# When the three expert loads into freed buffers are issued at the turn from mixer to experts

## The reference, cut to what matters

```python
for l in range(DEPTH):                      # DEPTH = 2
    ...
    x = x + merged @ w_out[l]
    x = x + hier_moe(rmsnorm(x, norm_ffn[l]), ...)

# hier_moe: 32 experts, top-1 group of 8, then the top 2 experts in it, per token
def expert_block(args):
    xb, e = args
    return (jax.nn.silu(xb @ w_gate[e]) * (xb @ w_up[e])) @ w_down[e]
```

## Time and profile before

| | |
|---|---|
| median of 3 runs | 1892.27 us (1889.84 to 1895.29) |
| the profiled execution | 1895.76 us |
| its span, first to last instruction | 1894.0 us |
| PE, DVE, ACT busy | 89%, 30%, 21% of the span |
| bytes moved by DMA | 496.44 MB, 262 GB/s over the span |

### The profile page before, as it was taken

One profiled execution on the slowest core, in us unless ns is written; L12 is line 12 of the kernel. 1 busy time (PEld: TensorE's weight loads), 2 busy tenths in 40 slices (PEclk: granted clock), 3 DMA queues, 4 the chain that ended last, 5 costly groups with the idle time before them and its releaser, 6 DMA issues.

```text
span 1894.0 us, 21754 instructions
## 1 busy us (share of the span) xinstructions
PE 1687.2 (89%) x7590; PEld 814.3 (43%) x7590; DVE 573.9 (30%) x1772; ACT 394.4 (21%) x961; POOL 80.9 (4%) x153
## 2 busy tenths in 40 slices
PE   7999999999998777777889999999999987787877
PEld 6664444444343323333376644444543432332332
DVE  4872345435100000000367623454350000000003
ACT  3322344111111111111113233441111111111111
POOL 1000000000010101010000000000000101010100
PEclk9999999999999989999989999999999999899999
DMA  5641110452999999999927311004529999999998
GB/s 165 146 138 45 30 38 23 178 244 76 421 426 426 426 427 428 427 427 426 381 65 184 100 45 45 23 23 178 244 105 427 427 428 426 426 426 428 427 426 333
DMA packets 121907, 496.44 MB, mean 262 GB/s; under 512 B 42036, under 2 KB 78900, under 8 KB 94160
## 3 DMA queue, kind: packets, MB, share of 16 engines
q1 hardware_dynamic: 109584, 472.75, 62.6%
q0 software_dynamic: 8928, 16.52, 2.3%
q10 hardware_dynamic: 3296, 5.84, 0.8%
HBM read 489.25 MB, written 30.47 MB: 274 GB/s over the span
## 4 chain that ended last, share of the span: by engine, by line
PE 61%; DMA 32%; DVE 3%; issue 2%; ACT 2%; SPq 0%; POOL 0%; DVEq 0%; ACTq 0%; POOLq 0%
PE bank L1071 15%; PE bank L739 14%; PE bank L762 13%; DMA arena<-in_expert_up 12%; DMA arena<-in_expert_gate 9%; DMA arena<-in_expert_down 7%; PE bank L966 6%; DMA hT<-in_expert_up 2%; PE bank L893 2%; PE bank L915 2%; PE bank L925 2%; PE bank L797 1%; PE bank L877 1%; ACT arena L1300 1%; DMA hT<-y_rows 1%
## 5 line engine op out<-in xcount | busy, mean ns | idle before, releaser
L1071 PE MATMUL bank<-arena 128*64 128x512 f32 x2176 | 679.7, 612 | 100.2 <-DMA arena<-in_expert_up 35.9
L1071 PEld LDWEIGHTS bank<-arena 128*64 128x64 f32 x2176 | 224.6, 141 | 358.9 <-issue 358.8
L1931 DVE SCALAR_TENSOR_TENSOR arena<-bank,halves,arena 128x512 f32<-128x512 f32 x32 | 24.0, 751 | 805.0 <-PE bank L1071 805.0
L762 PE MATMUL bank<-hT,arena 128*128 128x512 f32 x512 | 263.4, 613 | 2.8 <-ACT arena L1275 2.5
L1071 PE MATMUL bank<-h,arena 128*64 128x512 f32 x320 | 140.9, 622 | 29.3 <-DMA arena<-in_expert_gate 10.0
L1071 PE MATMUL bank<-spare_slot,arena 128*64 128x512 f32 x320 | 133.9, 616 | 30.2 <-DMA arena<-in_expert_gate 9.9
L739 PE MATMUL bank<-arena,hT 128*128 128x256 f32 (+1 forms) x512 | 122.3, 401 | 3.0 <-DMA arena<-in_w_in 2.2
L1071 PE MATMUL bank<-hT,arena 128*64 128x512 f32 x256 | 115.6, 605 | 0.0
L966 PE MATMUL bank<-arena,hT 128*128 128x512 f32 x256 | 115.0, 597 | 0.0
L739 PEld LDWEIGHTS bank<-arena,hT 128*128 128x128 f32 x512 | 101.3, 200 | 20.7 <-issue 2.6
L762 PEld LDWEIGHTS bank<-hT,arena 128*128 128x128 f32 x512 | 83.3, 192 | 55.6 <-issue 49.1
(11 more groups left out here) (349 smaller groups left out, 1617.2 us busy)
## 6 DMA issues: line engine op xcount, KB each, us to landing
arena<-in_expert_up SPq DMA_DIRECT2D x48, 2048.0 KB, 36.3
arena<-in_expert_gate SPq DMA_DIRECT2D x44, 2048.0 KB, 36.9
arena<-in_expert_down SPq DMA_DIRECT2D x44, 2048.0 KB, 38.7
arena<-in_w_in SPq DMA_DIRECT2D x26, 1024.0 KB, 7.6
spare_slot<-in_expert_gate SPq DMA_DIRECT2D x8, 2048.0 KB, 30.3
h<-in_expert_gate SPq DMA_DIRECT2D x8, 2048.0 KB, 31.9
hT<-in_expert_up SPq DMA_DIRECT2D x8, 2048.0 KB, 43.0
spare_slot<-in_expert_down SPq DMA_DIRECT2D x8, 2048.0 KB, 38.0
```

Source lines behind the costliest of these rows:

```text
L762: r = pe.matmul(bank[:, FB, :], lhs, rhs, start=(k == 0), stop=last)
L1071: r = pe.matmul(dst[CAP * e:CAP * e + CAP, :], moving[:, k, CAP * e:CAP * e + CAP], w, start=(k == 0), stop=(k == n - 1))
L1931: STT(hid, bank[:, 3, :], slot_root, hid, ALU.mult, ALU.mult).then_inc(act_ready, 1)
```

## The change

Load 7 is issued as soon as the projection is done, ahead of the wait for the stores. Load 8 is issued behind that wait, ahead of the wait for the first gather. Load 9 stays behind the gather.

```diff
                 sp.wait_ge(out_mm, 2 * NT)
                 leave(sp, left_mix)
+                load(7, 1)
                 sp.wait_ge(x_out, 32 * NT)
-                load(7, 1)
+                load(8, 1)
                 sp.wait_ge(rows_in, 16)
-                for i in range(8, NSLOT):
-                    load(i, 1)
+                load(9, 1)
                 sp.wait_ge(rounds_ready, 1)
```

## The result

The changed kernel took 1898.18 us (median of 11 runs, 1893.12 to 1902.14), the kernel before beside it 1894.00 us (11 runs, 1889.84 to 1898.60): a ratio of 1.0023, 95% interval 1.0013 to 1.0033. That is 4.4 us **slower**, where 1889.0 us, 0.17% faster, was forecast (from 1892.27 us for the kernel before, which now measures 1.7 us more). The two together say slower by 0.05 to 0.23%; the mean of the two ratios is 1.0014, 2.7 us.

What follows compares the result with a forecast made beforehand. Expert loads at 427 GB/s were taken to bound the kernel, held early by PE's slot frees. Gains of 1.6 and 1.7 us in the two layers, 3.3 us, took 1892.27 to 1889.0 us, range 1885.0 to 1894.8 us.

Steps and rivals of the forecast that it cites:

- What bounds the kernel: Expert stages: DMA loads set the pace at 427 GB/s, but early on PE's frees of slots decide when loads are issued.
- Part 1: Load 7 ahead of the stores: no gain in itself; stores land by 465.2 us at the latest, costing the gather's issue nothing.
- The cover: Time between the stores' late landing and the gather's issue at 468.8 us, which waits for the table: 3.6 us.
- Part 2: Load 8 ahead of the gather: the gather lands by 474.1 us at the latest, PE's delay taken as 0.
- late bound: Latest landing of the last tile's stores beside load 7, and so latest issue of load 8: 465.2 us.
- the prediction's own sign of being wrong: PE's first turning of rows over 1 us late, or the chain's first DMA piece ending over 3 us earlier.
- Part 3, the slack: Load 9 alone behind the gather: gains 1.6 and 1.7 us; queue slack at PE's frees caps gains at 2.2 and 2.3 us.
- such a restart: Load 10 starts on a queue run dry behind load 9, costing 1.3 us at most; later loads follow at once.
- A: Rival: the stream is not held at the frees, each layer gains 4.9 us, 1882.5 us; chance 7%.
- B: Rival: a single load delays store and gather as many do, PE turns rows 7.5 us late, 1902.8 us; chance 8%.
- C: Rival: nothing moves, as dry queue costs over 1.3 us or PE starts 1 to 2 us late, 1892.3 us; 15%.
- the prediction's 1.25 us: Delay of the last tile's stores if they share the engines with load 7 packet by packet, landing near 462 us.

Runs made afterwards that it cites:

- The two together: The changed kernel against the kernel before, measured in two sessions: ratio 1.0023, then 1.0005 (0.9994 to 1.0016).
- all loads late: The kernel before with loads 7, 8 and 9 all issued behind the first gather: ratio 1.0055, 10.4 us slower.
- The kernel with a late PE: The kernel before with 9 identity multiplications for 6 behind the table, loads' issue unmoved: ratio 1.0020 (1.0010 to 1.0029), 3.8 us slower.

## Why the prediction was wrong, point by point

- *What bounds the kernel*: right. Behind 507 us the changed kernel moves 425 and 427 GB/s in the windows of the earlier trace rows, and with all loads late the loss was one load a layer.
- *Part 1*: right in its end, though its bound was passed. The stores held `x_out` until 466.5 us, not 465.2: load 7 landed 10.0 us after its issue, at 465.7 us, and the small store 0.8 us behind it, 7.5 us after its own issue where 3 to 6 were forecast. The cover was put at 3.6 us and was 2.3; the gather's issue was not moved, and load 7 alone cost nothing.
- *Part 2 is the step that failed*: "A delay of PE is between 0 and 2 us, and I take 0." The gather landed at 475.4 us in layer 1 and not by 474.1, because load 8 began 1.3 us later than the late bound. Counted from A the gather landed at 8.8 us in place of 5.6, 3.2 us later, and in layer 2 as much. The slack between its landing and PE's turning of rows was 2.1 us before (474.15 - 472.05) and 1.7 us in layer 2, as claimed, and was overrun by 1.15 and 1.5 us. That is past the prediction's own sign of being wrong, a turning more than 1 us late. The rule of Part 2, that the gather lands at the latest with load 8 and 0.4 us for its own bytes, held: what it was fed, 465.2 us for `x_out`, didn't.
- *What was not in the sum at all*: the clock. Behind the wait the granted clock fell in layer 1 from 1.00 to between 0.54 and 0.60 for 4 us (not in layer 2, behind a wait as long), which added 1.5 us between turning rows and the first expert matmul (3.4 instead of 1.95 us). The forecast priced the wait and not what an idle PE does next.
- *Part 3, the slack*: mis-sized, the second step that failed. It was called 2.2 and 2.3 us. The kernel with a late PE measured 0.6 and 1.1 us by its stream, and the kernels with load 8 alone moved, where PE is on time, gained 0.4 to 1.0 us a layer by theirs, where 1.6 and 1.7 were forecast. Two terms were off, in opposite directions. More lay in the queue than the sum says: it took off two gathers of 0.18 MB, but three had moved 0.66 MB by then. SP's queue alone, 455 to 500.52 us of the kernel before:

```profile
q1 hardware_dynamic: 888, 13.01, 69.9%
```

That leaves 14.68 - 13.01 = 1.67 MB, 3.9 us and not 3.1. On the other side a new load costs more than 0.9 us for its first bytes, even where the queue still holds work: the rate can fall before that work is done. With 3.9 us left it hardly does. Windows of the kernel before, behind the issue at 500.52 us:

```profile
501.00:503.00 2.00, 2.00 (x12) 0.86 (x10) 0.00 (x0) 0.07 (x1) 0.77 (x2) 1.00 0.97 408
502.00:504.00 2.00, 2.00 (x12) 0.72 (x10) 0.00 (x0) 0.00 (x0) 1.02 (x1) 1.00 1.00 420
```

In the first kernel with load 8 alone moved 13.81 MB had gone by the same issue (499.38 us), so 2.0 us were left, and the rate fell:

```profile
501.00:503.00 2.00, 2.00 (x12) 0.81 (x10) 0.00 (x0) 0.00 (x0) 1.02 (x1) 1.00 0.82 254
```

The changed kernel has 10.49 - 10.03 MB, 1.1 us, left at 493.18 us and 14.68 - 13.60 MB, 2.5 us, at 503.26 us, and dips behind both:

```profile
494.00:496.00 2.00, 0.58 (x5) 0.42 (x5) 1.21 (x3) 0.60 (x1) 0.19 (x1) 1.00 0.81 246
...
505.00:507.00 2.00, 2.00 (x12) 0.86 (x10) 0.00 (x0) 0.00 (x0) 1.02 (x1) 1.00 0.96 340
```

So the stream loses with 2.5 us left and not with 3.9. The forecast charged such a restart to load 10 and let the bytes of loads 12 and 14 follow at once. What the start of a load costs in full, and why, no run here takes apart.

- *The rivals*: A, a full load saved, never came near. B named the right place, the gather, and the right test, its landing past 476 us; it came at 475.4, so B's price was far too high, but a milder B is what happened. C held its mechanism too ("PE starts 1 to 2 us late by the gather and the slack goes for that") and stopped at no loss, because it believed in 2.2 us of slack and had no term for the clock.

The sum as it now reads for layer 1: gather 3.2 us later, less 2.1 us of slack, makes 1.1 us; clock 1.5 us; together 2.6 us late at the first expert matmul (12.25 against 9.63 us), of which 2.1 us reach the stream of loads. In layer 2 PE is 1.5 us late and the stream 0.2 us: the earlier load 8 gives the rest back. That makes 2.3 us, against 4.4 us measured (2.5 to 6.2 by the interval) and 2.7 us by the mean of the two ratios; the second time the stream was 1.0 us late in all, and 0.9 us was measured. So the way from the gather to the stream is shown, and the full 4.4 us of the first measurement is not.

What stays open: why load 8 went out with a lead of 2.3 us over the gather in one execution and 3.1 in another, that is, why load 7 and the same stores were over 0.7 us sooner. The small store landed 0.8 us behind load 7 in every layer with load 7 alone ahead of the stores whose trace has both landings, and load 7 took 9.4 to 10.2 us; no kernel here varied that by itself.

## What to carry to other kernels

A load put into an idle stretch of the DMA queues is not free if a small transfer on the critical path is issued before the load has landed: the gather here then landed with the load. So count back from the small transfer's issue, and start the load early enough to be over, or start it behind. Where transfers are released one by one as an engine frees buffers, the queue's slack is what is left in it less the full start-up of the next load, and the start-up is best measured by holding the engine up on purpose, as the kernel with a late PE does. And where a wait is lengthened in front of TensorE, price the clock as well as the wait: two useless multiplications fewer cost 3 to 4 us here.

## What the runs showed of the hardware that was not expected

**A gather lands with the load issued before it, on another queue.** The gather moves 0.18 MB and landed at 475.37 us, 472.86 us and 475.84 us in three kernels, and load 8 at 466.54 + 8.7 = 475.24, 472.5 and 475.6 us: within 0.1 to 0.4 us. Load 8 of the changed kernel, as the tile's rows show it:

```profile
L655 SPq DMA_DIRECT2D arena<-in_expert_up x1: 333/333/333, 466.5 to 466.5; - x1
...
DMA to landing us min/median/max: 8.7/8.7/8.7
```

It is the gather's bytes that wait, and not only its semaphore. Alone, issued at 468.77 us, it moved all of them between 470.6 and 472 us (q0 is POOL's queue; kernel before):

```profile
q0 software_dynamic: 144, 0.18, 50.3%
```

In the changed kernel, issued at 468.88 us, it moved nothing up to 472.9 us, while load 8 had the engines to itself, and everything from then to 475.4 us, with load 8's last bytes. The queues from 468.9 to 472.9 us, then from 472.9 to 475.4 us:

```profile
q1 hardware_dynamic: 101, 1.65, 98.1%
```

```profile
q0 software_dynamic: 144, 0.18, 19.6%
q1 hardware_dynamic: 20, 0.07, 6.6%
```

**Stores beside a load take turns with it, packet by packet.** From 461 to 463 us of the changed kernel load 7 (q1) and the 512 KB store (q10, ACT's queue) moved:

```profile
q1 hardware_dynamic: 32, 0.52, 75.6%
q10 hardware_dynamic: 25, 0.10, 12.4%
```

That is 16 KB a packet for the load and 4 KB for the store: nearly as many packets, a fifth of the bytes. The 512 KB store took 7.8 us in place of 2.7 and landed 0.9 us before load 7, and the 8 KB store took 7.5 us in place of 1.4 and landed 0.8 us behind it; behind two loads it took 11.3 us. With three loads in front the 8 KB store landed 2.0 us before the last of them (13.9 us after its issue at 460.6 us, against 18.3 us after 458.2 us). So "lands with the load" holds for the gather and not for every small transfer.

The Trainium skill ("DMA: Bandwidth & Descriptors", Queues, rings and completion order) says that the semaphore increment lands only after earlier writes of the same DMA engine across its queues. No run here shows that this held anything up: the gather's own bytes were late, and the large store's semaphore came before that of the load in front of it. What the same section says of taking turns packet by packet agrees with the stores' rows above; the prediction's 1.25 us came of pricing the turns by bytes and not by packets. Why the gather found no turn beside load 8 stays open.

**The clock falls at an idle time that differs from run to run.** The granted clock fell to between 0.50 and 0.63 behind idle times of 2.6, 3.0, 3.2, 3.5 and 4.5 to 4.9 us and stayed at 1.00 behind 1.8, 2.1, 2.3 and, once, 3.1 us.
